# The first pair of groups behind each norm: whole fp32 weights and activations without the norm's factor

## The reference

```python
def rms_norm(x, g):
    y = x * lax.rsqrt(jnp.mean(x * x, axis=-1, keepdims=True) + NORM_EPS)
    return y * g

u = rms_norm(h, norm_mix_g[layer]);  p = u @ w_in[layer]      # ... mixers ...
h = h + merged @ w_o[layer]
u = rms_norm(h, norm_ffn_g[layer]);  h = h + conv_glu(u, w_up[layer], ...)
```

## Time and profile before

| | |
|---|---|
| median of three runs | 2048.01 us (2047.32 to 2049.75) |
| the profiled execution | 2048.42 us, its span 2046.5 us |
| TensorE matmul busy | 1883.6 us, 92% |
| VectorE busy | 1293.0 us, 63% |
| ScalarE busy | 1140.5 us, 56% |
| GpSimd busy | 1037.9 us, 51% |
| mean granted TensorE clock | 0.959 |

### The profile page before, as it was taken

How to read it: one execution, slowest core, us unless ns; L and a number is a source line. 1 busy time by engine, 2 the same in 40 slices (tenths; PEclk the granted TensorE clock), 3 DMA queues, 4 the chain that set the end, 5 groups by cost and what they waited for, 6 DMA issues and landing times.

```text
span 2046.5 us, 44566 instructions
## 1 busy us (share of the span) xinstructions
PE 1883.6 (92%) x16390; PEld 1778.9 (87%) x16390; DVE 1293.0 (63%) x1943; ACT 1140.5 (56%) x1924; POOL 1037.9 (51%) x742
## 2 busy tenths in 40 slices
PE   8889889999999889888999999988899998879999
PEld 8778779999999778778999989866899997669999
DVE  3487725669913397824669963476786536777764
ACT  5653455456755654445557755665555457465544
POOL 5663449839986573448929985741200045411000
PEclk9999989999999999979999999997999999779999
DMA  6432015656665432005656664420366653205665
GB/s 208 122 103 71 23 39 158 176 145 186 188 187 164 124 114 74 23 22 154 176 151 179 187 173 133 150 89 21 112 183 202 193 166 113 72 17 154 186 193 173
DMA packets 146922, 271.20 MB, mean 133 GB/s; under 512 B 16433, under 2 KB 16946, under 8 KB 146738
## 3 DMA queue, kind: packets, MB, share of 16 engines
q1 hardware_dynamic: 145296, 264.97, 45.2%
q10 hardware_dynamic: 1442, 3.66, 0.5%
HBM read 267.52 MB, written 1.05 MB: 131 GB/s over the span
## 4 chain that ended last, share of the span: by engine, by line
PE 65%; DVE 15%; ACT 9%; POOL 8%; issue 3%; DMA 0%; ACTq 0%; DVEq 0%; SPq 0%
PE bank L649 63%; POOL ring_split L1317 8%; ACT arena L1351 7%; ACT hi_ring L1351 1%; PE bank L758 1%; DVE arena L1891 1%; DVE u L1961 1%; DVE arena L1890 1%; DVE arena L2062 1%; DVE arena L1975 1%; DVE arena L1974 0%; DVE arena L2109 0%; DVE arena L1973 0%; ACT L1351 0%; DVE arena L2464 0%
## 5 line engine op out<-in xcount | busy, mean ns | idle before, releaser
L1317 POOL TENSOR_TENSOR ring_split<-ring,hi_ring 128x512 fp32r<-128x512 f32 x682 | 969.1, 1449 | 736.7 <-ACT hi_ring L1351 730.9
L1351 ACT ACTIVATE hi_ring<-ring 128x512 fp32r<-128x512 f32 x1002 | 619.3, 630 | 555.1 <-PE bank L649 532.0
L649 PE MATMUL bank<-u_hi,hi_ring 128*128 128x256 f32 (+1 forms) x2480 | 676.1, 285 | 47.3 <-POOL ring_split L1317 39.7
L649 PE MATMUL bank<-u_split,hi_ring 128*128 128x256 f32 (+1 forms) x2480 | 665.4, 281 | 1.6 <-DVE u_split L1966 1.4
L649 PE MATMUL bank<-u_hi,ring_split 128*128 128x256 f32 (+1 forms) x2480 | 665.0, 281 | 0.0
L649 PEld LDWEIGHTS bank<-u_hi,hi_ring 128*128 128x128 f32 (+1 forms) x2480 | 452.3, 188 | 61.8 <-POOL ring_split L1317 41.1
L649 PEld LDWEIGHTS bank<-u_split,hi_ring 128*128 128x128 f32 (+1 forms) x2480 | 452.4, 188 | 4.0 <-DVE u_split L1966 2.4
L649 PEld LDWEIGHTS bank<-u_hi,ring_split 128*128 128x128 f32 (+1 forms) x2480 | 452.2, 188 | 0.9
L1999 DVE TENSOR_TENSOR ring_split<-ring,hi_ring 128x512 fp32r<-128x512 f32 x320 | 215.3, 694 | 111.9 <-ACT hi_ring L1351 108.1
L649 PE MATMUL bank<-arena 64*64 64x64 f32 (+6 forms) x3680 | 240.3, 255 | 14.6 <-DVE arena L2109 9.3
L649 PEld LDWEIGHTS bank<-arena 64*64 64x64 f32 (+3 forms) x3680 | 210.4, 155 | 49.5 <-issue 29.7
(11 more groups left out here) (246 smaller groups left out, 2407.0 us busy)
## 6 DMA issues: line engine op xcount, KB each, us to landing
ring<-in_stream SPq DMA_DIRECT2D x1002, 256.0 KB, 2.8
par<-in_params ACTq DMA_DIRECT2D x3, 637.0 KB, 4.3
h<-in_x SPq DMA_DIRECT2D x4, 256.0 KB, 4.3
cst<-in_cst SPq DMA_DIRECT2D x1, 993.0 KB
out<-h ACTq DMA_DIRECT2D x3, 256.0 KB, 2.8
par<-in_params ACTq DMA_DIRECT2D x1, 633.0 KB, 8.3
out<-h ACTq DMA_DIRECT2D x2, 128.0 KB, 2.3
msk<-in_masks SPq DMA_DIRECT2D x1, 104.0 KB
```

Of the source, the lines that this page charges most:

```text
L649: ins = nc.tensor.matmul(o, l, r, start=start, stop=stop)
L1317: G.tensor_tensor(ring_lo[:, c, :], ring[:, c, :], hi_ring[:, q % HI_RING, :].bitcast(F32), ALU.subtract).then_inc(lo_by_pool, 1)
L1351: return nc.scalar.activation(o, i, f, **kw)
```

## The change

The eight first pairs no longer use split operands. ScalarE writes a copy of h times the gain, without the norm's factor (`gained_part`, one instruction for each k, behind the squares of each part), and TensorE multiplies it by the whole, unrounded pieces in fp32: `project_whole`, 32 matmuls of fp32 in place of 96 of fp32r. These 8 pieces are not split by any engine; a piece counts as ready when its DMA has landed. `norm_total` moves from before the pair to behind its first two k, and the 8 (or 16) matmuls of `keep_warm` go away. The norm's factor goes into the two full banks: VectorE multiplies them by it (`rescale` for A and U of the first kind, in place in the bank; for cq0 and ckv, and for U0 and U1 of the second kind, the product is written to where ScalarE wrote before, so ScalarE's two instructions there go away). ScalarE's reading of the first two banks of A and U waits for `raw_scaled`. `norm_parts` and `norm_hi` still make u for the third group and on; the third group waits for the parts of u one by one. The first piece behind the pair is now rounded before the parts of u, and the next three between them.

```diff
+WHOLE1 = {"A first", "A second", "U first", "U second"}
+WHOLE2 = {"cq first", "cq second", "U first", "U second"}
+BY_VECTOR1 = {"WO"}
+BY_VECTOR2 = {"WO", "D"} | {f"U{i}" for i in range(2, 16)}
...
+    def whole(self, q):
+        p, at = q // PIECE, q % PIECE * P
+        if p >= self.seen:
+            self.pe.wait_ge(self.landed[p % RING], (p // RING + 1) * 16)
+            self.seen = p + 1
+        return self.ring[:, p % RING, at:at + P]
...
+                def project_whole(names, act, parts, beside, with_ones=0):
                     open_ = [B.open(pe, name) for name in names]
-                    keep_warm(open_[0], warm)
                     for _ in range(with_ones):
                         mm(open_[0][:, 0:P], ones, ones)
                     q = W.take(names[0], 4 * KD)
                     W.ends[names[1]] = W.ends[names[0]]
+                    starts = [p_.start for p_ in PARTS]
                     for k in range(KD):
+                        if k in starts:
+                            pe.wait_ge(S["gained_parts"], parts + starts.index(k) + 1)
+                        for t in range(4):
+                            end = k == KD - 1 and t % 2 == 1
+                            mm(open_[t // 2][:, t % 2 * T:(t % 2 + 1) * T], W.whole(q + 4 * k + t), act[:, k, :], k == 0 and t % 2 == 0, end,
+                               full=names[t // 2] if end else None)
                         W.done(q + 4 * k + 3)
+                        beside(k)
...
-                project_first(("A0", "A1"), 0, 8 if l else 0, 0 if l else 16)
+                def total(k):
+                    if k == 1:
+                        norm_total("norm", next_squares, past["sums_ready"], (past["squares_ready"] - (l > 0), past["squares_ready"]))
+
+                project_whole(("A0", "A1"), next_whole, past["gained_parts"] - 5, total, 0 if l else 28)
                 for i in range(2, 7):
-                    project(f"A{i}", 2, u_parts)
+                    project(f"A{i}", 2, u_parts, ready=normed(0) if i == 2 else None)
...
+                def total1(k):
+                    if k == 1:
+                        norm_total("norm", next_squares, past["sums_ready"], (past["squares_ready"] - 1, past["squares_ready"]))
+                    if k == 2 and l == 0:
+                        norm_total("gained", gained, past["gained_sums"], (past["gained_ready"] - 1, past["gained_ready"]), ("gained_sums", "gained_ready"))
...
+            def gained_part(C, dst, gain, part_):
+                for k in range(part_.start, part_.stop):
+                    ins = A(dst[:, k, :], h[:, k, :], ACT.Copy, scale=gain[:, k:k + 1])
+                C.link(ins, S["gained_parts"])
+
+            def last_squares(C, dst, names, fresh, whole, gain, params_ready=None, last=False):
                 for j, (name, part_) in enumerate(zip(names, PARTS)):
                     hi.upto(name, HI_RING if j < 3 else LEAD)
                     act.wait_ge(S["h_ready"], past["h_ready"] + fresh + j + 1)
                     C.link(A(dst[:, part_, :], h[:, part_, :], ACT.Square), S["squares_ready"])
+                    gained_part(C, whole, gain, part_)
...
                     C.link(A(u_hi[:, part_, :], u[:, part_, :], ACT.Copy), S["u_hi_ready"])
-                    if j > 1:
-                        hi.make(at + HI_RING + j - 1)
+                    if j:
+                        hi.make(at + RING + j)
...
                     bank = B.wait(act, f"A{i // 2}")
+                    if i < 4:
+                        act.wait_ge(S["raw_scaled"], past["raw_scaled"] + i // 2 + 1)
...
-                hi.upto(LAST_WO[-1], HI_RING)
+                hi.upto(LAST_WO[-1], RING + 1)
                 norm_hi(C, 5, hi.ends[LAST_WO[-1]])
                 for i in range(23):
                     if i < 22:
                         hi.upto(f"U{i}")
                         bank = B.wait(act, f"U{i}")
+                        if i == 0:
+                            B.wait(act, "U1")
+                        if i < 2:
+                            act.wait_ge(S["raw_scaled"], past["raw_scaled"] + 2 + i + 1)
...
-                take_raw("cq0", cqk[:, 0:2, :], 2)
-                take_raw("ckv", cqk[:, 3:5, :], 2)
                 take_raw("cq1", cqk[:, 2:3, :], 1)
...
                     if j > 2:
-                        lo.make(at + HI_RING + j - 2)
+                        lo.make(at + RING + j - 2)
+
+            def rescale(C, B, names, factor):
+                for name in names:
+                    bank = B.wait(dve, name)
+                    C.link(V.tensor_tensor(v3(bank[:, :], 2), v3(bank[:, :], 2), spread(factor, 2), ALU.mult), S["raw_scaled"])
...
-                lo.upto("A0", 0)
+                rescale(C, B, ("A0", "A1"), rn[:])
...
                 norm_parts(C, p("g_ffn"), tmp, 5, lo.ends[LAST_WO[-1]])
-                lo.upto("U0", 0)
+                rescale(C, B, ("U0", "U1"), tmp)
...
+                    C.link(V.tensor_tensor(gained_scale, rn[:], buf, ALU.mult))
...
-                lo.upto("cq0", 0)
+                for n, o in (("cq0", 0), ("ckv", 3)):
+                    bank = B.wait(dve, n)
+                    C.link(V.tensor_tensor(cqk[:, o:o + 2, :], v3(bank[:, :], 2), spread(gained_scale if l == 0 else rn[:], 2), ALU.mult), S["raw_scaled"])
+                    B.release(dve, n)
...
                 for i in range(16):
                     lo.upto(f"U{i}")
-                    dve.wait_ge(S["conv_in"], past["conv_in"] + 4 + i + 1)
                     x_ = hidden[:, 2 * i:2 * i + 2, :].rearrange("p a t -> p (a t)")
+                    if i < 2:
+                        bank = B.wait(dve, f"U{i}")
+                        C.link(V.scalar_tensor_tensor(v3(x_, 2), v3(bank[:, :], 2), 0.0, spread(dn, 2), ALU.max, ALU.mult))
+                        B.release(dve, f"U{i}")
+                    else:
+                        dve.wait_ge(S["conv_in"], past["conv_in"] + 4 + i - 1)
                     C.link(V.tensor_tensor(x_, x_, x_, ALU.mult))
```

More of the change, by code:

```diff
@@ L368, in groups1, with groups2 @@
         g += [m2[0] for m2 in MERGE[i + 1:i + 2]] + [m[1]]
-    g += [*LAST_WO, "norm2"] + [f"U{i}" for i in range(22)] + ["D0"] + ["positions"] * last + [*LAST_D[1:], "norm"] + ["gained"] * last
+    g += [*LAST_WO, "U0", "U1", "norm2"] + [f"U{i}" for i in range(2, 22)] + ["D0"] + ["positions"] * last + [*LAST_D[1:]]
     return g
-def groups_head():
-    return ["norm"]
-def groups2():
-    g = ["cq0", "ckv", "cq1", "kpe", "aq", "ak", "ncq", "nckv", "av", "nq", "nk", "qk0", "qk1"]
+def groups2(first=False):
+    g = ["cq0", "ckv", "norm"] + ["gained"] * first + ["cq1", "kpe", "aq", "ak", "ncq", "nckv", "av", "nq", "nk", "qk0", "qk1"]
     g += ["uq0", "uq1", "uk0", "uk1", "uv", "rq", "rk", "nlq0", "nlq1", "nlk0", "nlk1", "if", "mv0", "mv1"]
@@ L389, in groups2 @@
     g += ["bn", "ln", "mn0", "mn1"]
-    g += [*LAST_WO, "norm2"] + [f"U{i}" for i in range(16)] + [*LAST_D, "norm"]
+    g += [*LAST_WO, "U0", "U1", "norm2"] + [f"U{i}" for i in range(2, 16)] + [*LAST_D]
     return g
@@ L606, in build @@
         omu = small[:, 64:78]
+        gains = small[:, 112:120]
         nbf = small[:, 80:81]
+        gained_scale = lgpt[:, 3 * T:4 * T]
         isz = small[:, 84:88]
         stage_banks, opened = [], 0
-        for kind in stages:
-            groups = (groups_head, groups1, lambda: groups1(True), groups2)[kind]()
+        for i, kind in enumerate(stages):
+            groups = (list, groups1, lambda: groups1(True), lambda: groups2(stages[i - 1] == LAST))[kind]()
             stage_banks.append(Banks(groups, banks, bank_full, bank_free, opened))
@@ L1710, in _ @@
                 last = l + 1 == layers[0]
-                last_squares(C, next_squares, LAST_D, 5, last)
-                guess_norm(C, B, "norm", "next")
-                hi.upto(LAST_D[-1], HI_RING)
+                last_squares(C, next_squares, LAST_D, 5, next_whole, gains if last else PAR1.of(par, "g_mix"), (stage + 1) * 16, last)
+                guess_norm(C, stage_banks[stage + 1], "norm", "next")
+                hi.upto(LAST_D[-1], RING + 1)
                 if last:
@@ L2570, in _ @@
                 if l + 1 < layers[1]:
-                    refine_norm(C, B, "norm", "next", 8, 1)
+                    refine_norm(C, stage_banks[stage + 1], "norm", "next", 8, 1)
 def lay_out(i):
```

179 lines of the change are left out of this document (83 added, 96 removed).

## The result

The changed kernel takes 2060.88 us, the median of 20 runs (2048.26 to 2069.97), against 2051.41 for the kernel before on the same chip (20 runs, one of which took 5204.23 us); ratio 1.0043, 95% interval 1.0026 to 1.0059. Slower by 0.4%, where 2044.2 us and faster was forecast. A second measurement, on another chip with six runs of the changed kernel, gave 1.0076 (1.0052 to 1.0100). The profiled execution took 2066.07 us (span 2064.3) with a mean granted clock of 0.949; the earlier trace rows are of one of 2048.42 us at 0.959.

What follows compares the result with a forecast made beforehand. It took TensorE's stream, broken at hand-overs such as the eight norms, as the bound. Gains 0 x 4 + 0.9 + 1.5 + 2 x 1.4 less 1.4 gave 3.8 us, hence 2044.2 us; 8-in-10 range 2034 to 2051.

Steps and rivals of the forecast that it cites:

- The pair on TensorE: First pair at each norm: 64 fp32 rows at 0.216 us, 13.8 us; third group begins at 15.6 after TensorE leaves WO or D.
- The norm's factor 3.5 us later: At the norms: sum over squares ends at 5.2 instead of 1.7; last part of u ready at 18.0, 0.3 to 0.5 stall.
- Behind the pair: Norms one to four: ScalarE waits for VectorE's rescaling, so fifth piece comes at 25.2 (U) or 23.3 (A); gain 0 each.
- Second kind of U: Norms six and eight, VectorE makes all remainders: late piece at 22.3, TensorE idles 2.5 us, gain 1.4 us each.
- The last D stage: Last D stage of the first kind: ScalarE's extra copies lengthen TensorE's idling, cost 1.4 us (ends 0.9 and 2.8).
- The sum at full clock: Whole kernel: 0 x 4 + 0.9 + 1.5 + 2 x 1.4 - 1.4 = 3.8 us gained.
- Norm seven: At ckv, where ScalarE no longer reads the banks: 2.0 less 0.5 of stall, gain 1.5 us.
- the start: First norm: pair ends at 27.3 instead of 29.2 us, but the wait behind it leaves a gain of 0.
- its own first part: Opening on what bounds the kernel: some 4.5 us at each norm carry nothing, including 3.6 us of matmuls on constants.
- The slower one: Rival: VectorE and GpSimd alternate strictly, last part of u at 20 or later; 2055 us, half of it 2051; chance 0.17.
- Clean: Rival: ports hardly meet, last part of u at 15.4 to 16, banks rescaled when the pair ends; near 2036 us; chance 0.28.
- too dear: Rival: fp32 pair takes 0.24 us a row, 15.4 us; cost 3 to 4, 2047 to 2048 us, no change; chance 0.10.

## Why the prediction was wrong

- **The pair on TensorE: right.** 0.213 us a row (0.216 forecast), 13.6 for the pair's 64 rows (13.8); the third group starts at t = 15.35 (15.6).
- **The norm's factor 3.5 us later: right,** guess at 5.4, the last part of u at 17.5 (18.0); the new meeting of VectorE and GpSimd cost 1.9 at one place instead of 2 x 1.3.
- **Behind the pair: right in time for U** (24.8 against 25.2), 1 us too early for A (24.1 at norm three, 23.3 forecast). But the forecast gave the rescaling as what holds ScalarE. The run without it says a third of the gap.
- **Second kind of U:** the late piece at 22.9 and 23.3 (22.3), idling 2.97 and 3.33 (2.5), so the gain at full clock is 0.8 and 0.6, not 1.4 each. The last D stage: 0.6 to 0.8 more idling instead of 1.4, but the stage is 2.0 us longer, and the first one, which the forecast left out, 1.6.
- **The sum at full clock: near, by terms that partly cancel.** By the 81st blocks the norms gain about 3 us (4.7 at two to eight, less 1 to 2 at the start), and the longer gap in the last D stage takes 0.7, which leaves 2 to 3; 3.8 was forecast. Norm seven gave 2.1 (1.5), the second kind of U less than forecast, and the start, put at 0, lost. Another measure, span times mean clock, is weaker than it looks: it gives 1965.7 us over 23 runs of before and 1960.5 over six of after, but also 1960.5 for the kernel before without its filler, which has nothing to gain at full clock. Low clock beside a wait costs less than this product counts.
- **The step that failed** is the pricing of gaps in "Behind the pair" and in "U of the second kind": a stall was counted at its own length, and one as long as the gain before it as 0. The forecast wrote that TensorE would idle 2 to 4 us at six norms and gave the matmuls behind it the full clock. They lost it: 24 to 31 us at half speed, which cost 9 to 12 us of time where 0 stood in the sum, three times what the edit gained. Of the difference in the profiles this is the largest part, D's 3.6 us and the mixers are the rest. The hint stood in its own first part: 3.6 us of matmuls on constants where TensorE waits, and a clock of 1.00 beside them. The forecast took these matmuls to "carry nothing". The run without them says 22 us. The pricing failed, not the timeline: where the waits would open and how long they would be was forecast within 1 us.
- **Rivals.** The slower one (2051 to 2055, by strict alternation of the ports, gaps above 5 us) named another mechanism, and the measured time is beyond it too: no gap behind a pair was above 3.6, and at norm two only one of the later parts of u was stretched at length. Clean didn't come: the last part of u was there at 17.5, not before 16. The pair was not too dear. None of the rivals held the clock.

## What to carry over

Price an idle gap of TensorE as its length and what the clock takes behind it; here some 3 us of idling mostly cost 1.4 to 2.7 us more. Put filler only where a timeline shows a wait (5 matmuls at a place without one cost their whole 2.0 us), and look at the stages behind it too. When an edit moves work into a place with filler, look at where the idling goes, since the filler doesn't go with it. The edit was sound once the next gap was closed in ScalarE's order: with that and two small edits it beats the kernel before by 0.36% (0.21 to 0.51).

## What the runs showed of the hardware

What idling does to the clock is not a matter of one gap's length. In the three profiles of the changed kernel it fell behind all twelve gaps of 2.96 to 3.59 us (norms two, four, six and eight), and behind two of the six of 2.65 to 2.89 (norms one and three). Behind 1.9 us (norms two and four) it stayed up in the kernel before, but fell in the same kernel without its filler, where a gap of 4.56 us had come 19 us earlier, and at the third norm it fell behind 1.81 us in the kernel without rescaling. At the fifth norm gaps of 1.8 and 2.5 us, 1 us of work between them, brought 6.8 us of low clock in all three. Each fall behind a norm lasted 3.4 or 6.8 us and cost 1.4 to 1.7 or 2.0 to 2.7.

The Trainium skill (TensorE: Matmul & The Clock Gate, Part 1: The HAM clock gate) says that the gate follows how busy the engine has been and that its phase differs between executions of one kernel. The third norm agrees: 2.73 us brought the clock down in one profile of the changed kernel, 2.74 and 2.89 did not in the others.
